# The sample tile's projections in pairs of 64-column halves, with the gates spread between its chains and the samples' queries turned two pages later

## What is computed

```python
z = _rmsnorm(x, g_pre) @ w_in
(cq, ckv, kpe, gate_mla, gq, gk, gv, gg, gate_gla, mq, gate_mem) = _split_in(z)
q = jnp.einsum('blr,rhd->blhd', _rmsnorm(cq, g_qa), w_uq)
q = _rope_tail(_rmsnorm(q, g_mla_q), pos)
ckv = _rmsnorm(ckv, g_kva)
...
gla_g = (jax.nn.log_sigmoid((gg @ w_gk + b_gk).astype(jnp.float32)) / GLA_NORMALIZER)
mem_q = _rmsnorm(mq.reshape(b, L, MEM_HEADS, MEM_HEAD_DIM), g_mem_q)
...
# samples: attention over the paged cache, page by page, with a running maximum
k = _mla_keys(c_blk, kpe_blk, pos, w_uk, g_k)
sc = jnp.einsum('bthd,bphd->bhtp', q, k).astype(jnp.float32) * MLA_SCALE
```

## Time and profile before

| | |
|---|---|
| median of 3 runs | 2792.41 us (2791.17 to 2795.13) |
| profiled execution | 2792.35 us, span 2790.6 us |
| PE busy | 2748.2 us, 98% of the span |
| DVE busy | 1890.6 us, 68% |
| ACT, POOL busy | 880.7 us (32%), 329.6 us (12%) |
| chain that ended last | PE 86%, DVE 9%, ACT 2% |

### The profile page before, as it was taken

How to read it: one execution, slowest core, us unless ns; L and a number is a source line. 1 busy time by engine, 2 the same in 40 slices (tenths; PEclk the granted TensorE clock), 3 DMA queues, 4 the chain that set the end, 5 groups by cost and what they waited for, 6 DMA issues and landing times.

```text
span 2790.6 us, 54559 instructions
## 1 busy us (share of the span) xinstructions
PE 2748.2 (98%) x17973; PEld 1619.7 (58%) x17973; DVE 1890.6 (68%) x3801; ACT 880.7 (32%) x1903; POOL 329.6 (12%) x467
## 2 busy tenths in 40 slices
PE   8999999999999999999999999999999999999999
PEld 4666677765455555555466667777545555555553
DVE  3666655567898888886245666566488888888842
ACT  1333333342333333332013333333323333333300
POOL 0111100002111111110010000001021111111100
PEclk9999999999999999999999999999999999999999
DMA  7222223325444444544532222233353444445422
GB/s 289 73 65 68 70 72 74 75 65 175 113 111 128 130 114 128 174 132 136 210 123 60 64 70 68 72 75 72 98 162 103 126 123 130 119 136 183 118 100 87
DMA packets 528940, 313.70 MB, mean 112 GB/s; under 512 B 360009, under 2 KB 512146, under 8 KB 525586
## 3 DMA queue, kind: packets, MB, share of 16 engines
q1 hardware_dynamic: 526912, 309.41, 38.6%
q10 hardware_dynamic: 1746, 0.81, 0.1%
HBM read 287.63 MB, written 89.60 MB: 135 GB/s over the span
## 4 chain that ended last, share of the span: by engine, by line
PE 86%; DVE 9%; ACT 2%; issue 1%; DMA 0%; POOL 0%; SPq 0%; DVEq 0%; ACTq 0%
PE ps L1918 29%; PE ps L1512 13%; PE ps L1997 8%; PE ps L1937 4%; PE ps L1746 4%; PE ps L1949 4%; PE ps L1506 3%; PE ps L1711 3%; PE ps L1771 2%; PE ps L1518 2%; PE ps L1523 2%; PE ps L1931 1%; ACT U L730 1%; PE ps L1718 1%; DVE w_in L1396 1%
## 5 line engine op out<-in xcount | busy, mean ns | idle before, releaser
L875 ACT ACTIVATE w_in<-ps 128x512 f32<-128x512 f32 x512 | 305.7, 597 | 688.1 <-PE ps L1918 629.4
L1918 PE MATMUL ps<-w_uk,region 128*128 128x512 f32 x1040 | 470.2, 596 | 0.0
L1396 DVE TENSOR_REDUCE w_in<-w_in 128x8 f32<-128x512 f32 x512 | 351.2, 686 | 48.8 <-ACT w_in L875 32.7
L1512 PE MATMUL ps<-w_in,xT 128*128 128x256 f32 (+6 forms) x1360 | 378.3, 431 | 2.2 <-DMA w_in<-in_w_in 1.6
L1918 PEld LDWEIGHTS ps<-w_uk,region 128*128 128x128 f32 x1040 | 187.0, 190 | 216.5 <-issue 216.2
L1512 PEld LDWEIGHTS ps<-w_in,xT 128*128 128x128 f32 (+1 forms) x1360 | 246.4, 185 | 113.1 <-issue 69.3
L1918 PE MATMUL ps<-w_uk,xT 128*128 128x512 f32 x672 | 304.4, 596 | 0.0
L604 POOL TENSOR_TENSOR rs<-us,mhalf 128x1 f32<-128x1 f32 (+4 forms) x132 | 130.9, 991 | 1331.2 <-DVE us L1034 729.0
L1918 PEld LDWEIGHTS ps<-w_uk,xT 128*128 128x128 f32 x672 | 120.7, 190 | 136.8 <-issue 135.9
L1918 PE MATMUL ps<-w_uk,W 128*128 128x512 f32 x336 | 151.8, 593 | 1.0 <-ACT w_in L875 1.0
L1746 PE MATMUL ps<-region,W 96*128 96x512 f32 (+3 forms) x384 | 146.8, 494 | 0.1
(11 more groups left out here) (403 smaller groups left out, 4048.4 us busy)
## 6 DMA issues: line engine op xcount, KB each, us to landing
pages_by_quarter<-in_cache_ckv SPq DMA_DIRECT2D x512, 128.0 KB
region<-pages_by_quarter SPq DMA_DIRECT2D x80, 512.0 KB, 4.0
region<-in_cache_ckv SPq DMA_DIRECT2D x320, 128.0 KB, 2.2
w_in<-pages_by_quarter SPq DMA_DIRECT2D x48, 512.0 KB, 4.0
w_in<-in_cache_ckv SPq DMA_DIRECT2D x192, 128.0 KB, 2.1
w_in<-in_w_in SPq DMA_DIRECT2D x16, 1240.0 KB, 11.1
mix_quarters<-xn SPq DMA_DIRECT2D x16, 512.0 KB, 3.2
region<-in_cache_kpe SPq DMA_DIRECT2D x512, 16.0 KB
```

Source lines behind the costliest of these rows:

```text
L875: tell(act.activation(sqb[j % 4], ps[:, j if k == 0 and j < 2 else 2 + j % 2, :], ACT.Square), s.pkn_sq, np_)
L1396: tell(dve.tensor_reduce(pst[:, 0, j * H:j * H + H], heads(sqb[j % 4], H), X, ALU.add), s.pkn_red, np_)
L1512: ins = mm(out, xT[:, k, 0:T], w_in[:, k, c0:c0 + w], start=k == 0, stop=k == KD - 1)
L1918: ins = mm(ps[:, key_bank(k, j), :], page[:, o_:o_ + P], w_uk[:, c, :], start=c == 0, stop=c == 1)
```

## The change

- **Pairs.** gv and mq of the sample tile become one loop (`project_gv_mq`) whose matmuls alternate between partitions 0 to 63 and 64 to 127 of bank 5. It stands where gv stood (h = 6). ckv and cq become a pair too (banks 2 and 3), at the place of ckv. In q, the two halves of the heads alternate between the column halves. ACT and DVE read the upper partitions accordingly (the square of q, one instruction before, is two).
- **gq** of the sample tile moves to h = 7 of tile 7, ahead of the last head's outputs; before, mq stood there.
- **Gates.** The eight steps, before 1 and 7, stand as 2 (before the sum of the decay), 2 (before the transposes of ck), 1 (before q) and 3 (at the end).
- **Queries.** In the first group the steps on PE at j = 1, 2, 5 go to j = 3, 4, 7, those on DVE at j = 2, 3, 6 to j = 3, 4, 7, and DVE's fills from j = 7 to j = 6.

```diff
+                def project_pair(lo, w_lo, hi, w_hi):
+                    for k in range(KD):
+                        a_lo = mm(lo, xT[:, k, 0:TS], w_in[:, k, w_lo[0]:w_lo[0] + w_lo[1]], start=k == 0, stop=k == KD - 1)
+                        a_hi = mm(hi, xT[:, k, 0:TS], w_in[:, k, w_hi[0]:w_hi[0] + w_hi[1]], start=k == 0, stop=k == KD - 1)
+                    return a_lo, a_hi
+                def project_gv_mq(L=L):
+                    pe.wait_ge(s.xT_evac, 2 * (NT * L + TP) + 2)
+                    for a_ in project_pair(ps[0:TS, 5, 0:GW + GR], (O_GV, GW + GR), ps[TS:2 * TS, 5, 0:MW], (O_MQ, MW)):
+                        a_.then_inc(s.gvmq_ps, 1)
...
+                            a_ckv, a_cq = project_pair(ps[0:TS, 2, 0:R + ROPE], (O_CKV, R + ROPE), ps[TS:2 * TS, 3, 0:QR], (O_CQ, QR))
...
-                    else:
-                        project(ps[0:T, 3, 0:QR], T, O_CQ, QR).then_inc(s.cq_ps, 1)
+                    if not pm_:
+                        project_gates(0, 2)
                     pe.wait_ge(s.g_ready, n + 1)
...
+                    if not pm_:
+                        project_gates(2, 4)
                     pe.wait_ge(s.ck_ready, n + 1)
...
-                        project_gates(0, 1)
+                        project_gates(4, 5)
                     pe.wait_ge(s.cqT_evac, n + 1)
...
+                            for e in range(2):
+                                ins = mm(ps[TS * e:TS * e + TS, 2 + e, 0:4 * QK], cqT[:, c, 0:T], w_uq[:, c, 4 * QK * e:4 * QK * e + 4 * QK], start=c == 0, stop=c == 2)
...
                             if h == 6:
-                                project_gv(t + 1)
+                                if t + 1 < TP:
+                                    project_gv(t + 1)
+                                else:
+                                    project_gv_mq()
                             if h == 7:
-                                project_mq(t + 1)
+                                if t + 1 < TP:
+                                    project_mq(t + 1)
+                                else:
+                                    project_T(ps[:, 4, 0:TS], TS, O_GQ, GKD)
...
                     intra_gla()
-                    project_gates(1, KD).then_inc(s.gates_ps, 2)
+                    project_gates(5, KD).then_inc(s.gates_ps, 2)
...
-                    if k == 0 and j == 2:
+                    if k == 0 and j == 3:
                         dve.wait_ge(s.qnT_ps, 2 * L + 1)
...
-                    if k == 0 and j == 3:
+                    if k == 0 and j == 4:
                         dve.wait_ge(s.qnT_ps, 2 * L + 2)
...
-                    if k == 0 and j == 6:
+                    if k == 0 and j == 7:
                         dve.wait_ge(s.qt_ps, L + 1)
...
-                    if k == 0 and j == 7:
+                    if k == 0 and j == 6:
                         own(dve.memset(acc[64:128, :, :], 0.0))
                         own(dve.memset(m0[64:128, :], NEG))
...
-                    if k == 0 and j == 5:
+                    if k == 0 and j == 7:
                         pe.wait_ge(s.qnT_evac, L + 1)
```

More of the change, by code:

```diff
@@ L701, in _ @@
                     act.wait_ge(s.gvmq_ps, 2 * n + 2)
-                    tell(act.activation(qk[0:T, 0, 0:MW], ps[0:T, 6, 0:MW], ACT.Square), s.mq_ss, n)
+                    tell(act.activation(qk[0:T, 0, 0:MW], ps[0:T, 6, 0:MW] if pm_ else ps[TS:2 * TS, 5, 0:MW], ACT.Square), s.mq_ss, n)
                     act.wait_ge(s.ckv_ps, n + 1)
@@ L715, in square_cq @@
                         act.wait_ge(s.cq_ps, n + 1)
-                        tell(act.activation(qk[0:T, 1, 0:QR], ps[0:T, 3, 0:QR], ACT.Square, accum_out=st[0:T, 2:3]), s.ssq_ready, n)
+                        tell(act.activation(qk[0:T, 1, 0:QR], ps[0:T, 3, 0:QR] if pm_ else ps[TS:2 * TS, 3, 0:QR], ACT.Square, accum_out=st[0:T, 2:3]), s.ssq_ready, n)
                     if not pm_:
@@ L755, in _ @@
                     act.wait_ge(s.mean_ready, mean(n, M_K) + 1)
-                    tell(act.activation(sq[0:T, 0:H * QK].rearrange("p (c n) -> p c n", c=2), ps[0:T, 2:4, 0:H * QK // 2], ACT.Square), s.q_sq, n)
+                    if pm_:
+                        tell(act.activation(sq[0:T, 0:H * QK].rearrange("p (c n) -> p c n", c=2), ps[0:T, 2:4, 0:H * QK // 2], ACT.Square), s.q_sq, n)
+                    else:
+                        own(act.activation(sq[0:TS, 0:4 * QK], ps[0:TS, 2, 0:4 * QK], ACT.Square))
+                        tell(act.activation(sq[0:TS, 4 * QK:8 * QK], ps[TS:2 * TS, 3, 0:4 * QK], ACT.Square), s.q_sq, n)
                     if pm_:
@@ L1114, in _ @@
                     dve.wait_ge(s.root_ready, mean(n, M_CQ) + 1)
-                    tell(ts(cq[0:T, :], ps[0:T, 3, 0:QR], rs[0:T, 2:3], None, ALU.mult), s.cq_ready, n)
+                    tell(ts(cq[0:T, :], ps[0:T, 3, 0:QR] if pm_ else ps[TS:2 * TS, 3, 0:QR], rs[0:T, 2:3], None, ALU.mult), s.cq_ready, n)
                     if n == 0:
@@ L1619, in _, with project_gates @@
                         project_mem(1, 0)
+                    def project_gates(k0, k1):
+                        for k in range(k0, k1):
+                            wide = w_in[:, k, O_GGLA:O_GGLA + 3 * GW].rearrange("p (a n) -> p a n", n=GW)[:, 0::2, :]
+                            mm(ps[0:TS, 7, :], xT[:, k, 0:TS], w_in[:, k, O_GMLA:O_GMLA + H * VD], start=k == 0, stop=k == KD - 1)
+                            ins = mm(ps[TS:2 * TS, 7, :].rearrange("p (a n) -> p a n", n=GW), xT[:, k, 0:TS], wide, start=k == 0, stop=k == KD - 1)
+                        return ins
                     pe.wait_ge(s.gg_ready, 2 * n + 1)
@@ L1660, in _ @@
                     ins.then_inc(s.cT_ps, 1)
[L1662 to L1668, removed]
                     def intra_gla():
@@ L1706, in _ @@
                     else:
-                        project_gates(0, 1)
+                        project_gates(4, 5)
                     pe.wait_ge(s.cqT_evac, n + 1)
-                    for e in range(2):
+                    if pm_:
+                        for e in range(2):
+                            for c in range(3):
+                                ins = mm(ps[0:T, 2 + e, 0:4 * QK], cqT[:, c, 0:T], w_uq[:, c, 4 * QK * e:4 * QK * e + 4 * QK], start=c == 0, stop=c == 2)
+                    else:
                         for c in range(3):
-                            ins = mm(ps[0:T, 2 + e, 0:4 * QK], cqT[:, c, 0:T], w_uq[:, c, 4 * QK * e:4 * QK * e + 4 * QK], start=c == 0, stop=c == 2)
+                            for e in range(2):
+                                ins = mm(ps[TS * e:TS * e + TS, 2 + e, 0:4 * QK], cqT[:, c, 0:T], w_uq[:, c, 4 * QK * e:4 * QK * e + 4 * QK], start=c == 0, stop=c == 2)
                     ins.then_inc(s.q_ps, 1)
```

18 lines of the change are left out of this document (12 added, 6 removed).

## The result

The changed kernel takes 2799.82 us (median of 20 runs, 2795.01 to 2805.16) against 2792.19 us before (20 runs, 2791.17 to 2796.04): 1.0028 times as long, 95% interval 1.0022 to 1.0034. It is slower by 7.6 us. Forecast were 2794.9 and a range up to 2799.0, so the median lies 0.8 us above the range. The profiled execution of the changed kernel took 2795.3 us (span 2793.5), near the fastest of its 20 runs. It shows where most of the added time goes, but not all of it.

What follows compares the result with a forecast made beforehand. DVE's chain, not PE, was taken to bound the sample tile and first group. Gains less the later queries' cost gave 0.9 us faster, 2791.5; plus 3.4 us of clock, 2794.9 us, range 2788 to 2799 (8 in 10).

Steps and rivals of the forecast that it cites:

- what bounds the kernel where the change touches it: Sample tile and first group: DVE's chain bounds into the second group; PE is the bound again from 693.77.
- Rival C: PE is the bound all the same and its 18.6 us are won: 2773.7 us; chance 0.04.
- D: Rival: column halves of unequal width or in two banks run one after the other: 2803.4 us, 0.4% slower; chance 0.05.
- What of it arrives at DVE: Sample tile to cosines' product: of PE's saving DVE's chain gains 1.9 us in the first layer, 2.5 in the second.
- step (5): Cosines' product: held by the cosines' transfer until 656.4 in the first layer, gaining 1.9 us; second layer gains 2.5.
- What the later queries cost: First group: scores 2.94 us later in DVE's time, 1.17 swallowed by PE's idle time, so 1.77 us late less the gain.
- Rival B: PE does not wait for `qt_ready`, so the stage's whole gain of 4.4 us counts: 2788.0 us; chance 0.08.
- A: Rival: the clock stays up, or falls early enough in the idle piece to be back: 2791.5 us; chance 0.25.
- What that idle piece does to the clock: About 5.4 us idle before the scores brings one fall to half clock, costing 1.7 us a layer, 3.4 in all.
- own range: The forecast's own range without rivals: 2792 to 2797 us, for 0.5 to 2.8 us of clock a layer.
- rival E: Clock also falls at the wait for q, down through two stretches a group, 3.4 us or more a layer: 2798 to 2800; chance 0.08.

Runs made afterwards that it cites:

- e6: The changed kernel measured and profiled once more, nothing altered: 2799.87 us (4 runs), ratio 1.0024 to the kernel before; its profiled execution took 2804.17 us.
- e5: The changed kernel with 5 unused matmuls of 512 columns (4.3 us) in PE's wait before the first group's scores: 2794.63 us against 2792.73, ratio 1.0007.
- e3: The changed kernel with 11 unused matmuls of 512 columns (9.7 us) in PE's wait before the first group's scores: 2802.51 us, ratio 1.0032 to the kernel before.
- e10: e9 with the change's later order of the queries' steps, but the four copies and PE's small matmuls at j = 6: 2790.27 us, ratio 0.9988.
- e2: The kernel before with only the first group's steps moved as in the change, no pairs or gates: 2803.97 us, ratio 1.0040.
- e4: The changed kernel with DVE's two fills moved into its wait in the sample tile, behind mq's norm: 2793.90 us, ratio 1.0003 to the kernel before.
- e9: The changed kernel with old first-group order, fills in the sample tile, sines' product in DVE's wait for the keys' root, tables told ready earlier: 2795.20 us, ratio 1.0006.
- e11: e10 with POOL's rotation of the first page waiting for qn_ready instead of table_ready: 2782.50 us against 2792.47 before, ratio 0.9966.

## Why the prediction was wrong

**Right**: what bounds the kernel where the change touches it. PE's 11.7 us fewer did not arrive, and DVE's chain set the scores. (Of the 18.6 us that PE was to save the busy time shows 11.7; the lower clock takes part of the rest back.) Rival C is out, and so is D: the pairs cost their wider member.

**"What of it arrives at DVE"** holds to some tenths. The wait for gg's copy was 0.53 us (forecast 0.7). The transfer of the quarters held DVE, though it landed at 642.4 and not 642.7. The copy of the decay's sum stood at 643.51 (643.9). Only step (5) did not bind: the cosines had landed before DVE asked for them, so the product gained 2.3 us in the first layer (1.9 forecast) and 2.7 in the second (2.5).

**"What the later queries cost"** holds as well. The fills and the reduction stand ahead of the four copies, PE waits 5.51 us for them (5.4 forecast), and the scores start 0.69 and 0.26 us later, counted from tile 7 (1.04 and 0.44 forecast). The sum without the clock was 0.9 us faster. The first trace, its falls taken out of the two stages, gives 1.7 faster, e6's trace 1.4 faster. By medians it is less good: e5, without the falls, is 1.9 us slower than before (0.6 faster to 4.7 slower by its interval). Rival B is out, and so is A: the clock did not stay up.

**"What that idle piece does to the clock"** is the step that failed, by its size and not by its mechanism. I took one fall of 3.4 us with all of it on PE's work, 1.7 us a layer, because the one row there was had that the earlier trace rows. The medians have 2.6 to 3.6 a layer (e5), and of traced layers 3.3, 3.3, 4.2 and 5.8. Two things are missing from my term. A second fall comes behind the small matmuls and costs another 1.7 (a fall of 3.4 us at half clock); the row of the first prompt tile has none, and no such matmuls stand there. And the falls last longer in other executions, up to 17 us, while the scores and the 8-column matmuls run. The first fall alone came out nearly as I sized it: 6.8 us long, 3.7 of them on work, 1.85 us. With 2.6 to 3.6 in place of 1.7 a layer the sum would have been 2796.7 to 2798.7. The last 1 to 3 us up to 2799.82 are not accounted for; the interval of e5 alone is 2.7 us to either side.

The bound was set with the same fault. I wrote "3.4 us if it lasts twice as long", from one fall doubled (the "0.5 to 2.8 us of clock a layer" of the own range is no better worked out: 2792 is 0.25 a layer), and so put rival E at 2798 to 2800 with a chance of 0.08. Its time came true (2799.82), its place did not: neither trace of the changed kernel has a fall at the wait for q. What comes near it is the fall that lasts on through the scores, 12.7 us of work in e6. So the time of E is luck. An effect seen once should have carried a range to more than twice its size: the 5.8 us a layer that one traced layer has would be 2803.

A rule of the Trainium skill (TensorE: Matmul & The Clock Gate, "HAM oscillation — how this bites in real kernels") has each burst of matmuls behind a long wait start cold. This case's traces agree for the first fall (0.50 at 681.39, 1.00 in e5 with the wait filled). They show a second fall of which that section says nothing.

## What to carry to other kernels

An idle piece of PE is not free where PE is the bound soon after it: here 2.4 to 5.5 us of waiting cost 3.0 to 5.8 us of clock on top. So a step that is moved later in order to hide a chain has to be moved with what stands ahead of it: the later order cost 10.5 us with the fills ahead of the last copies, 3.8 with the fills out of the way, and gained 4.9 only when the sines' product was out of the way too and the copies stood a page earlier (which of the two did it was not tried apart). Try it with the work put ahead of the chain first, then with the order, and when a wait of another engine is loosened, look at the durations beside it and not only at the starts.

## What the runs showed of the hardware

- The clock fell a second time although PE was busy for all of 3.40 of 3.40 us by the records (685.10 to 688.50, 24 matmuls of 8 columns among them), and in another execution stayed at 0.50 for 12.7 us with PE busy for 12.68. A busy PE in the profile doesn't mean a clock that stays up. In e3 it fell behind the same small matmuls in both layers with no wait of PE in the 20 us before. The kernel before, e5 and e10 run them too, in both layers of their traces at 1.00. So the small matmuls don't always bring it; what decides is not settled.
- Behind the wait before the scores the clock was at 0.50 in both layers of all four traces that have 2.4 to 5.5 us of idle time there (the changed kernel's two, e2's and e4's; in the second layer of e2 from 0.5 us behind the start of the scores), and at 1.00 in both layers of e5, with 1.0 us of the wait left.
- DVE and POOL slow each other in SBUF. In e9, 0.28 us became 0.43 and 0.50, 0.42 became 0.79 and 0.83, 0.68 became 1.10, and one copy 1.31, beside a fill of 1.80 us on POOL; the three copies behind it kept their 0.28; on POOL 0.46 became 0.90. DVE's stream transposes and reductions kept their durations beside POOL's rotation in e11 (1.10 and 1.11 us, three reductions in 2.13), and the cosines' product, with two inputs in SBUF, its 1.22 us beside a fill on POOL (657.65 and 658.52 in e11).
- The Trainium skill (SBUF — State Buffer, "Who interferes with whom") says that a DVE instruction with two SBUF inputs contends with a GpSimd instruction that reads SBUF, that copies can contend, that reductions do not, and that of a DVE instruction in a two-port mode, which a copy can enter, and a GpSimd instruction the one that comes second is blocked whole. The first three agree with e9 and e11. The last agrees with the one copy of 1.31 us, which starts 0.64 us behind POOL's fill and ends just after it; in which mode the copy ran the records don't say. The products grow less, up to twofold on either side.
